# Reordering a two-block kernel: band scores ahead of a v panel, a residual ahead of a weight split, four modulation panels moved into the triangular solve

## What is computed

```python
mod = (silu(c) @ w_ada + b_ada)                       # six vectors of 1024, "modulation"
shift_t, scale_t, gate_t, shift_f, scale_f, gate_f = split(mod, 6)
h = x * (1 + scale_t) + shift_t
qkv_a, z_a, beta, a, q_b, k_b, v_b, gates = split(h @ w_in)
o_a = gated_deltanet(qkv_a, z_a, beta, a, ...)        # (A + I) x = rhs per head: a triangular solve
o_b = chunk_band_attention(q_b, k_b, v_b, rel_bias)   # 16 heads of 64
merged = gate_a * (o_a @ w_branch_a) + gate_b * (o_b @ w_branch_b)
x = layernorm(ALPHA * x + gate_t * (merged @ w_o))
u = causal_dwconv(h' @ w_up); x = layernorm(ALPHA * x + gate_f * (silu(u_gate) * u_val) @ w_down)
```

## Time and profile before

| | us |
|---|---|
| three timed runs | 1074.77, 1076.4, 1079.91 (median 1076.4) |
| the profiled execution, its own time | 1082.24 |
| its span, first to last instruction | 1080.5 |
| PE, DVE, ACT busy | 995.9, 704.3, 551.0 |
| mean granted clock of PE | 0.956 of full speed |

### The profile page before, as it was taken

One profiled execution on the slowest core, in us unless ns is written; L12 is line 12 of the kernel. 1 busy time (PEld: TensorE's weight loads), 2 busy tenths in 40 slices (PEclk: granted clock), 3 DMA queues, 4 the chain that ended last, 5 costly groups with the idle time before them and its releaser, 6 DMA issues.

```text
span 1080.5 us, 19933 instructions
## 1 busy us (share of the span) xinstructions
PE 995.9 (92%) x8478; PEld 932.1 (86%) x8478; DVE 704.3 (65%) x1098; ACT 551.0 (51%) x830; POOL 26.9 (2%) x70
## 2 busy tenths in 40 slices
PE   4897999979999999699999999899988889999996
PEld 1477999869999999599798998798988779999995
DVE  2659947547777765697864343366569678888843
ACT  2658521555444533566645435366734466666433
POOL 2010000000000000220100000000000000000000
PEclk7898999999999999799999999899988989999999
DMA  8642675536788888246432125453468615655930
GB/s 317 213 139 75 225 266 179 182 129 216 270 276 289 263 296 272 67 149 242 136 118 79 63 88 137 137 176 117 137 194 297 250 66 188 189 186 185 314 123 39
DMA packets 57113, 196.79 MB, mean 182 GB/s; under 512 B 6064, under 2 KB 10560, under 8 KB 56768
## 3 DMA queue, kind: packets, MB, share of 16 engines
q1 hardware_dynamic: 51552, 187.72, 52.1%
q10 hardware_dynamic: 5216, 7.53, 2.4%
q0 software_dynamic: 256, 0.26, 0.1%
HBM read 194.43 MB, written 1.06 MB: 181 GB/s over the span
## 4 chain that ended last, share of the span: by engine, by line
PE 79%; DVE 9%; ACT 6%; DMA 3%; issue 2%; SPq 0%; ACTq 0%; DVEq 0%
PE panel_banks L400 64%; DMA raw<-in_panels 3%; DVE w_lo L1477 2%; PE work_banks L613 2%; PE work_banks L785 2%; ACT w_hi L968 1%; DVE raw L1510 1%; PE panel_banks L453 1%; PE work_banks L572 1%; PE work_banks L714 1%; PE work_banks L756 1%; PE work_banks L545 1%; PE work_banks L868 1%; PE work_banks L487 1%; PE work_banks L813 0%
## 5 line engine op out<-in xcount | busy, mean ns | idle before, releaser
L400 PE MATMUL panel_banks<-act_hi,w_hi 128*128 128x256 f32 (+1 forms) x1600 | 467.4, 292 | 34.3 <-DVE w_lo L1477 15.2
L400 PE MATMUL panel_banks<-act_hi,w_lo 128*128 128x256 f32 (+1 forms) x1600 | 457.7, 286 | 0.0
L400 PE MATMUL panel_banks<-act_lo,w_hi 128*128 128x256 f32 (+1 forms) x1600 | 457.4, 286 | 0.0
L1477 DVE TENSOR_TENSOR w_lo<-raw,w_hi 128x1024 fp32r<-128x1024 f32 x260 | 315.3, 1222 | 169.3 <-ACT w_hi L968 168.7
L968 ACT ACTIVATE w_hi<-raw 128x1024 fp32r<-128x1024 f32 x260 | 272.3, 1054 | 169.3 <-PE panel_banks L400 127.0
L400 PEld LDWEIGHTS panel_banks<-act_hi,w_hi 128*128 128x128 f32 x1600 | 307.6, 192 | 48.5 <-issue 29.3
L400 PEld LDWEIGHTS panel_banks<-act_lo,w_hi 128*128 128x128 f32 x1600 | 308.0, 193 | 2.0 <-issue 0.5
L400 PEld LDWEIGHTS panel_banks<-act_hi,w_lo 128*128 128x128 f32 x1600 | 307.8, 192 | 1.5
L400 PE MATMUL panel_banks<-hidden_hi,w_hi 128*128 128x256 f32 x352 | 98.5, 280 | 2.4 <-ACT hidden_hi L1185 2.4
L1510 DVE CUSTOM_DVE_ANT_0 raw<-raw,c_wide 128x1024 f32<-128x1024 f32 x80 | 94.5, 1220 | 8.1 <-DMA raw<-in_panels 8.1
L400 PE MATMUL panel_banks<-hidden_lo,w_hi 128*128 128x256 f32 x352 | 98.5, 280 | 0.0
(11 more groups left out here) (269 smaller groups left out, 1021.4 us busy)
## 6 DMA issues: line engine op xcount, KB each, us to landing
raw<-in_panels SPq DMA_DIRECT2D x356, 512.0 KB, 5.1
mix_work<-delta_rows ACTq DMA_DIRECT2D x2, 1024.0 KB, 10.9
x_t<-in_x ACTq DMA_DIRECT2D x1, 1024.0 KB, 9.3
gla_work<-in_ctx_x ACTq DMA_DIRECT2D x1, 1024.0 KB, 14.4
mix_work<-in_rel_bias ACTq DMA_DIRECT2D x1, 1024.0 KB, 8.1
out_x<-ffn_work SPq DMA_DIRECT2D x2, 512.0 KB, 2.6
mix_work<-in_rel_bias ACTq DMA_DIRECT2D x1, 768.0 KB, 13.7
c_wide<-in_c_rows ACTq DMA_DIRECT2D x1, 512.0 KB, 16.7
```

What stands on the lines that cost most here:

```text
L400: ins = pe.matmul(out_, a, b, start=start and p == 0, stop=stop and p == 2, skip_group_check=True)
L1477: dve.tensor_tensor(wlo[:, v_ % PARTS, :], raw[:, u % RAW, :], whi[:, v_ % PARTS, :].bitcast(F32), ALU.subtract)\
```

## The change

- `LAYERS`: the four A panels of branch_b go to band_q, one behind each S panel. The A panels of mix stay.
- `SOLVE_ROWS`: DVE does one `accumulate_half` after `tend` at steps 0, 1, 3, 5, 7, 9, 11 and 13 of the solve. In exchange the `accumulate()` at ("a", 2) and ("a", 3) and those at i = 0 and 1 of the merge loop are gone. An `accumulate()` is two halves, so there are eight moved, and as many in all as before.
- `FILL["delta_norm"]` goes from 64 to 60: band_scores(0) is issued before the last band_v panel (quarters 60 to 63). `tend("scores")` on ACT and DVE thereby stops four quarters earlier.
- The last `residual` of mix is called before `lower_parts(j + 2)` instead of behind it.

```diff
@@ -43,8 +43,8 @@
 LAYERS = [("mod_first", "R", 8), ("gla_k", "S", 2), ("gla_q", "S", 2), ("gla_r", "S", 4),
           ("gla_v", "SAA", 4), ("mods", "A", 4), ("gla_out", "S", 4), ("ffn_in", "SSA", 11),
           ("ffn_out", "SSA", 5), ("ffn_out_rest", "S", 1), ("qkv", "S", 12), ("z", "S", 4),
-          ("band_q", "S", 4), ("band_k", "S", 4), ("band_v", "S", 4), ("gates", "S", 8),
-          ("branch_a", "S", 4), ("branch_b", "SA", 4), ("mix", "SA", 4), ("up", "S", 22),
+          ("band_q", "SA", 4), ("band_k", "S", 4), ("band_v", "S", 4), ("gates", "S", 8),
+          ("branch_a", "S", 4), ("branch_b", "S", 4), ("mix", "SA", 4), ("up", "S", 22),
           ("down", "SA", 4), ("down_rest", "S", 7)]
 
 
@@ -92,13 +92,14 @@
 
 SOLVE = ["A", "N2", "N2T", "T2", "N4", "N4T", "T4", "N8", "T8", "T", "U", "W", "T", "U", "W", "T", "U", "W"]
 ADDED = [p for p, name in enumerate(SOLVE) if name in ("T2", "T4", "T8", "W")]
+SOLVE_ROWS = (0, 1, 3, 5, 7, 9, 11, 13)
 TURN_VALUES = {0: 0, 4: 1, 8: 2, 12: 3}
 
 
 FILL = {"k_sums": 5, "q_sums": 10}
 FILL.update({("product", _r): 10 + _r for _r in range(1, 6)})
 FILL.update({(0, _p): 16 + _p for _p in range(18)})
-FILL.update({"begun": 36, "predicted": 39, "corrected": 42, "delta_out": 48, "delta_sums": 56, "delta_norm": 64,
+FILL.update({"begun": 36, "predicted": 39, "corrected": 42, "delta_out": 48, "delta_sums": 56, "delta_norm": 60,
              "scores": 68})
 for _i in range(8):
     FILL.update({("pair", _i): 70 + 4 * _i, ("rest", _i): 72 + 4 * _i})
@@ -1890,6 +1891,8 @@
                         dve.tensor_tensor(s_n[t], s_a[t], over_tiles((d32, d64)[p // 11], 8), ALU.mult)\
                             .then_inc(S(f"masked{t}"), 1)
                 tend((0, p))
+                if p in SOLVE_ROWS:
+                    accumulate_half()
                 if p == 14:
                     dve.wait_ge(S("panel_evacuated"), first["band_k"][1] - 1)
                     for t in range(2):
@@ -1961,8 +1964,6 @@
                 if n == 1:
                     dve.wait_ge(S("ob_hi"), 1)
                     lower(flat(hlo[:, 0:8, :]), flat(ob), flat(hhi[:, 0:8, :]), "ob_lo")
-                else:
-                    accumulate()
             tend("ended")
             j += 28
             def merge(i):
@@ -1989,7 +1990,7 @@
             for i in range(4):
                 if i < 3:
                     lower_parts(j + 2)
-                if i < 3:
+                if i == 2:
                     accumulate()
                 merge(i)
                 if i:
@@ -1999,10 +2000,13 @@
             lower_parts(j + 1)
             accumulate()
             for i in range(4):
+                if i == 3:
+                    residual(first["mix"][1], i)
                 lower_parts(j + 2)
                 if i < 2:
                     accumulate()
-                residual(first["mix"][1], i)
+                if i < 3:
+                    residual(first["mix"][1], i)
                 j += 1
 
             def layer_norm(count, gain, after=None):
```

## The result

The kernel after takes 1063.0 us (median of 4 runs, 1059.05 to 1071.94), the kernel before 1078.2 us in the runs beside it. The ratio is 0.988, with a 95% interval of 0.985 to 0.991, which is 13 us of 1078. Forecast were 12.1 us and 1064.3.

The account below looks back on a forecast made before the run. The prediction took PE as the bound, busy 995.9 of 1080.5 us, with its idle and half-clock time to win. Terms 2.3 - 0.6 + 9.3 + 1.1 = 12.1 us, from 1076.4 to 1064.3 us; range 1057.5 to 1070.5.

Parts of the forecast that it names:

- 2.3 of clock: Mix: half clock behind the stop ahead of mix, 13.6 us for 11.3 us of work, would go; 2.3 us won.
- -2.9 at residual 0: Mix: PE would wait 2.5 us on residual(0) instead of 0.38, plus 0.8 for a clock drop; 2.9 us lost.
- 2.0 at residual 3: End of mix: residual(3) ahead of the split lets norm_part(3) run 2 us earlier.
- the centring behind the splits: First layer norm: two splits now precede the centring on DVE, so only 1.1 of the 2 us stay.
- Part 1: Band: first scores ahead of the last v panel win 7.1 us, less a new 2.95 us stop and 1.8; net 2.3.
- the drop behind the new stop: Band, after band_scores(1): the new 2.95 us stop is followed by half clock, costing 1.8 us, ends 0 and 3.7.
- Part 2: Solve: eight accumulate calls fit under PE's work except at step 13, delaying step 14's adds; 0.6 us lost, bounds 0 and 2.
- Part 3: Branch_b and mix without half of the accumulates: 7.4 + 4.8 - 2.9 = 9.3 us won, bounds 4.5 and 12.
- Part 4: End of mix: residual(3) ahead of the split wins 1.1 us net, bounds 0.5 and 2.
- Late panels at residual 0 with the lower clock behind it: Rival in mix: accumulate panels land late, residual(0) stops PE 6 us with 3.7 of half clock; 1070.7 us, chance 0.12.
- The hidden transfer: Rival in branch_b: ACT's late sigmoid makes the stop, A panels only filled the gap; gain about 5, 1071.5 us, chance 0.06.
- The solve starved of transfers: Slower rival in the solve: A halves land late, DVE waits eight times, 30 us; 1094 us, chance 0.03.

Follow-up runs that it names:

- The doubled load: Kernel after with one more DVE pass of 128x1024, without transfer, behind each of the eight accumulates in the solve; solve stretch 106.7 us against 103.8.
- the run with the splits to 64: Kernel after with ACT and DVE again splitting ahead to 64 behind the first scores, PE's order kept; 1060.6 us, ratio 0.983 to the kernel before.
- part 4 alone: Kernel before with only residual(3) of mix put ahead of the split; 1076.9 us beside 1080.5 of the kernel before.
- part 1 alone: Kernel before with only FILL delta_norm at 60, so band_scores(0) precedes the last v panel; 1075.8 us, ratio 0.998 (0.995 to 1.001).

## Why the prediction was right, step by step

**The whole.** 13 us measured, 12.1 forecast; direction and size were right, and each stop that was named appeared where it was named. The time of 1063.0 for 1064.3 is nearer than the terms are: it was worked out from 1076.4 us for the kernel before, whose median in the comparison was 1078.2. The forecast's terms, put on the stretches of the table above (us gained):

| stretch | forecast | measured |
|---|---|---|
| solve | -0.6 | -0.6 |
| band | 2.3 | 4.4 |
| to mix (7.4, and 3.21 - 0.7 ahead of mix) | 9.9 | 9.5 |
| mix (2.3 of clock, -2.9 at residual 0, 2.0 at residual 3) | 1.4 | 2.1 |
| first layer norm (the centring behind the splits) | -0.9 | 0.5 |
| sum | 12.1 | 15.8 |

The sum of the stretches is above the 13 us of the timed runs, whose interval is 9.5 to 16.5. Three stretches came out better than forecast, by 2.1, 0.7 and 1.4 us, mostly through the clock, which falls differently from run to run; how near the whole came to 12.1 is in part luck.

**Part 1.** Forecast a gain of 2.3 us, measured 4.0 alone and 4.4 in the kernel after. The stops were right (5.30 gone, 2.94 new for 2.95). Mis-sized was the clock: I booked the drop behind the new stop at 1.8 us on top of everything else. A drop there does cost nearly that (24 matmuls in 4.60 us for 3.03 to 3.07), but it came only where the 2.25 us stop ahead of it isn't followed by the lower clock. The band of before had 10.2 us at the lower clock, behind both stops, and 3.0 of them fell into the 5.30 us stop itself; those of both kernels with part 1 have 3.4. So some 3.8 us less of PE's work ran at the lower clock, worth 1.9, and the shorter stop gives 2.4, together 4.3 of the 4.4. With the moved panels alone, where the 2.25 us stop wasn't followed by the lower clock, the band takes 92.8 us, and against that part 1 is worth 3.1. Why there is no second drop stays open; the upper bound, 4.2, was the one without it. The working also lists the 2.87 us stop at 856.81 as one without a drop; its first matmuls are at full clock, but from 859.2 on, in the next stop, the clock is at the lower level for 6.8 us.

**Part 2.** Forecast 0.6 us lost, measured 0.6 to 0.7, from step 14's adds, as named: with the last accumulate at step 12 the stretch is back at 103.1 us. The doubled load shows that the cover of steps 6 and 8 was as thin as worked out.

**Part 3.** Branch_b ran without a stop and at full clock, as worked out. The moved panels alone gave 8.5 us in time (5.3 to 11.6) for 9.3. Ahead of mix PE waits 0.49 us where I had 0.7, on residual 0 1.98 where I had 2.5. The 2.5 hides a slip: 11.0 us of queue from 819.4 end at 830.4, not at 829.7, which would be a stop of 3.2. The queue took 9.9 us (807.26 to 817.12), because DVE no longer waits 1.04 us for ACT in it. Not foreseen was 1.01 us on residual 1, behind a half that landed late (ACT's wait of 6.45 us). In mix no lower clock followed, for which I had added 0.8; in the run with the splits to 64 it did, for 3.4 us. The size was right, but one reason was not: I put the stop ahead of mix to DVE's full queue. With DVE's work taken out and the transfers left it is 5.18 us, so it too came from halves that land late, which held DVE's in-order queue, with the merges in it, as well as ACT.

**Part 4.** Forecast 1.1 us, measured 1.2 in waits, by the mechanism named. That the layer norm gained 0.5 instead of losing 0.9 is the clock again: 3.4 us at the lower level for 8.5. With part 4 alone, where it has 8.6 us at that level, it takes 15.0 us, 0.7 more than before.

**The rivals.** Late panels at residual 0 with the lower clock behind it: no, 1.98 us and a clock of 1.00 in mix; but a late half did come one panel further, ahead of residual 1, so ACT's wait for landing fell from 26.4 to 8.8 us and not well under 10. The hidden transfer: no; without the sigmoid the stops remain. The solve starved of transfers: no wait of DVE for an A half shows in the solve, its waits there are for ACT and PE. Of the rule of the Trainium skill on idle gaps between bursts (TensorE: Matmul & The Clock Gate, Why this matters for your kernels), which warns of long ones, the runs say both: the same 2.94 us stop was followed by the lower clock in the kernel after (24 matmuls in 4.60 us) and not with part 1 alone (3.06 us), and shorter ones, of 2.25 and 1.99 us, were followed by it in some of the traces.

**What stays open.** Where in a program the lower clock falls isn't settled by the length of a stop. Nor was it tried which of the ring's six slots would have to be free for branch_b to run with its A panels. So it isn't shown whether the panels landed late because more was asked for than the DMA engines move, or because slots came free late. For the stop in branch_b the trace of before speaks rather for the slots: from 786 to 802 the DMA engines are busy for 0.65 of the time, and SP waits there for DVE's splits to free slots, up to 8.6 us at a time:

```profile
786.00:802.00 16.00, 12.31 (x106) 12.13 (x104) 9.75 (x14) 6.37 (x8) 0.00 (x0) 0.97 0.65 198
```

From 802 to 824, ahead of mix, the share is 0.89. The experiment that takes DVE's work out keeps its waits for A halves, so it doesn't separate the late A halves from the S halves queued behind them. The profiled runs differ by up to 9 us in the untouched first half (563.2 to 572.5); I didn't look into it.

## What to carry to other kernels

Put transfers that one stage can't feed under a stage that has DMA and DVE to spare, and check the cover per step: one pass of 1.15 us fitted under a 1.4 us quarter in seven of the eight places, and two passes came too late in three of them. When a product is moved ahead of its cover, look at what the other engines' look-ahead is tied to: here the same table entry held back the splits, and freeing them was worth 4.5 us of the band. Give what a stop costs in clock as a range: the same stop was followed by the lower clock in one trace and not in another. To tell work from transfers, run one without the other: eight cheap passes with all transfers left 7.8 us of stops, eight full passes without transfers brought back only 2 us.

## What the runs showed of the hardware

The lower clock comes behind some stops and not others of the same length, in the same code. The stop of 2.25 to 2.34 us ahead of the band is in all thirteen traces; the lower clock followed it in seven. Behind the 2.94 us stop 24 matmuls took 4.60, 4.60, 4.59 and 4.47 us in four traces (the kernel after twice, the one with DVE's work, the one with the residuals first), and 3.06 and 3.07 in two, part 1 alone and the doubled solve load:

```profile
707.02 3.07 PE panel_banks L401 x24
```

In these two the clock had already fallen behind the 2.25 to 2.34 us stop 32 us earlier, and in the other four it had not: each of the six has one drop, behind one stop or the other. At the 5.30 us stop the clock was at the lower level in all five traces that have it. In mix a stop of 1.98 or 1.99 us cost no clock in three traces (the kernel after twice, the moved panels alone), nor did one of 2.61 us with the doubled solve load; one of 1.99 us in the run with the splits to 64 was followed by 3.4 us at the lower level (granted 0.57 over 4 us), and so was one of 2.56 us with DVE's work put back:

```profile
819.82:823.82 4.00, 4.00 (x17) 3.65 (x18) 1.87 (x2) 2.73 (x4) 0.00 (x0) 0.57 1.01 399
```

In the kernel before the stops of branch_b fall differently from run to run: 3.69 and 3.21 us in one trace, 1.65, 0.83, 0.92 and 4.10 in another with the same code in that stretch, at 57.0 and 54.9 us. And 563 to 572 us of identical work ahead of the solve held 37.5 to 54.6 us at the lower clock.
